# Two-layer decoder trunk on one Trainium2 core: the least used expert comes last, its 64 high and 64 low token parts in one stationary block

## What is computed

```python
def moe_swiglu(h, w_router, w_gate, w_up, w_down):
    logits = (x @ w_router).astype(jnp.float32)
    top_logit, top_idx = lax.top_k(logits, TOP_K)          # TOP_K = 2 of N_EXPERTS = 8
    gates = jax.nn.softmax(top_logit, axis=-1)
    ...
    return swiglu(xb, w_gate[e], w_up[e], w_down[e])       # (silu(h @ w_gate) * (h @ w_up)) @ w_down
```

## Time and profile before

| | |
|---|---|
| median of 3 runs | 1447.54 us (1447.46 to 1451.54) |
| profiled execution | 1448.84 us, of which the span of instructions 1447.0 us |
| PE busy | 1417.0 us, 98% of the span |
| DVE, ACT, POOL busy | 1116.4 us (77%), 944.6 us (65%), 52.8 us (4%) |
| 336 expert slots: DVE subtract, ACT copy | 2286 ns and 1915 ns each |
| DMA in the expert stage | 346 to 398 GB/s by slices of 36 us |
| indirect stores of token rows, issue to landing | 10.4 us |

### The profile page before, as it was taken

How to read it: one execution, slowest core, us unless ns; L and a number is a source line. 1 busy time by engine, 2 the same in 40 slices (tenths; PEclk the granted TensorE clock), 3 DMA queues, 4 the chain that set the end, 5 groups by cost and what they waited for, 6 DMA issues and landing times.

```text
span 1447.0 us, 19532 instructions
## 1 busy us (share of the span) xinstructions
PE 1417.0 (98%) x7348; PEld 1201.7 (83%) x7348; DVE 1116.4 (77%) x865; ACT 944.6 (65%) x866; POOL 52.8 (4%) x78
## 2 busy tenths in 40 slices
PE   8999999999998999999999999999999999999997
PEld 8887999998887888888888888888888888888886
DVE  5565544546775888798888889879888888987987
ACT  5654544335664867787677777767768768677774
POOL 1000100000000500000000000000000000000002
PEclk9999999999999899999999999999999999999999
DMA  9743665555531699999999999999999999999993
GB/s 283 265 146 116 252 228 187 193 191 177 185 117 59 213 397 395 397 393 395 393 354 395 396 346 394 398 349 392 396 391 347 395 393 346 393 398 352 396 396 136
DMA packets 205253, 446.72 MB, mean 309 GB/s; under 512 B 8448, under 2 KB 42400, under 8 KB 205200
## 3 DMA queue, kind: packets, MB, share of 16 engines
q1 hardware_dynamic: 200144, 428.34, 80.5%
q0 software_dynamic: 5056, 17.66, 3.5%
HBM read 432.86 MB, written 13.11 MB: 308 GB/s over the span
## 4 chain that ended last, share of the span: by engine, by line
PE 90%; DVE 3%; ACT 3%; DMA 2%; issue 1%; SPq 1%; DVEq 0%; ACTq 0%
PE ps L1686 28%; PE ps L1688 28%; PE ps L1687 28%; PE ps L2300 2%; DMA raw<-in_w_exp_down_dram 1%; DMA raw<-in_w_mem_kv_dram 1%; ACT w_hi L593 1%; ACT e_whi L977 1%; DVE w_lo L1058 1%; PE ps L2243 0%; PE ps L1835 0%; PE ps L2294 0%; ACT sc L637 0%; DVE small L1105 0%; PE ps L1712 0%
## 5 line engine op out<-in xcount | busy, mean ns | idle before, releaser
L1567 DVE TENSOR_TENSOR e_wlo<-raw,e_whi 128x2048 fp32r<-128x2048 f32 x336 | 752.6, 2286 | 103.0 <-ACT e_whi L977 102.9
L977 ACT ACTIVATE e_whi<-raw 128x2048 fp32r<-128x2048 f32 x336 | 622.9, 1915 | 53.2 <-PE ps L1688 26.2
L1686 PE MATMUL ps<-e_whi,act_hi 128*128 128x512 f32 x1344 | 529.4, 394 | 0.7 <-DVE act_lo L1580 0.7
L1688 PE MATMUL ps<-e_wlo,act_hi 128*128 128x512 f32 x1344 | 523.9, 390 | 0.0
L1687 PE MATMUL ps<-e_whi,act_lo 128*128 128x512 f32 x1344 | 523.2, 389 | 0.0
L1688 PEld LDWEIGHTS ps<-e_wlo,act_hi 128*128 128x128 f32 x1344 | 252.3, 188 | 53.3
L1686 PEld LDWEIGHTS ps<-e_whi,act_hi 128*128 128x128 f32 x1344 | 252.4, 188 | 52.0 <-DVE e_wlo L1567 1.4
L1687 PEld LDWEIGHTS ps<-e_whi,act_lo 128*128 128x128 f32 x1344 | 252.6, 188 | 50.6
L1058 DVE TENSOR_TENSOR w_lo<-raw,w_hi 128x2048 fp32r<-128x2048 f32 (+3 forms) x69 | 148.7, 2167 | 118.8 <-ACT w_hi L593 118.5
L593 ACT ACTIVATE w_hi<-raw 128x2048 fp32r<-128x2048 f32 (+3 forms) x69 | 124.3, 1816 | 47.2 <-PE ps L1688 43.5
L982 ACT ACTIVATE act_hi<-ps 128x512 fp32r<-128x512 f32 x56 | 33.5, 598 | 155.2 <-PE ps L2300 155.2
(11 more groups left out here) (270 smaller groups left out, 966.1 us busy)
## 6 DMA issues: line engine op xcount, KB each, us to landing
raw<-in_w_exp_gate_dram SPq DMA_DIRECT2D x112, 1024.0 KB, 9.3
raw<-in_w_exp_up_dram SPq DMA_DIRECT2D x112, 1024.0 KB, 9.5
raw<-in_w_exp_down_dram SPq DMA_DIRECT2D x112, 1024.0 KB, 10.1
raw<-in_w_dense_gate_dram SPq DMA_DIRECT2D x11, 1024.0 KB, 5.3
raw<-in_w_dense_up_dram SPq DMA_DIRECT2D x11, 1024.0 KB, 5.6
raw<-in_w_dense_down_dram SPq DMA_DIRECT2D x11, 1024.0 KB, 6.7
raw<-in_w_out_dram SPq DMA_DIRECT2D x8, 1024.0 KB, 5.0
raw<-in_w_in_a_dram SPq DMA_DIRECT2D x7, 1024.0 KB, 11.9
```

Of the source, the lines that this page charges most:

```text
L977: nc.scalar.activation(e_whi[:, (s - NPRE) % E_SPLIT, :], raw[:, s % RAW, :], ACT.Copy)\
L1567: nc.vector.tensor_tensor(e_wlo[:, r, :], raw[:, s % RAW, :], e_whi[:, r, :].bitcast(F32), ALU.subtract).then_inc(lo_ready, 1)
L1686: nc.tensor.matmul(dst, l_hi, r_hi, start=start, stop=False)
L1688: return nc.tensor.matmul(dst, l_hi, r_lo, start=False, stop=stop)
```

## The change

- After the counts are known, DVE sorts the experts: expert 0 stays first, the others follow by falling count (`order_of`, `place`). SP reads the number of the next expert from SBUF before it issues that expert's loads; POOL's row numbers use `place`, so they wait for `routed` in place of `ranked`. If the last expert has over 64 tokens, its ranks from 64 on are moved past 128, so that the second sweep runs.
- The last expert (`light`) has its at most 64 tokens' high parts in stationary columns 0 to 63 and their low parts in columns 64 to 127 (`pack`). Each product is then two matmuls of 512 columns, times the high and the low weights. Rows 0 to 63 and 64 to 127 of the result are its two halves, to be summed.
- For the hidden block the sum is made in the turning: ACT copies the gate product and DVE the up product to SBUF, and PE multiplies both with `fold` (two 64-wide identities, one on the other), 8 matmuls of 64 columns (`light_turn`). ACT takes the silu of the turned gate, DVE multiplies by the turned up part, ACT writes the high part, DVE the low part beside it. For the output the sum is made in the scatter, whose one-hot columns stand twice.

The diff, cut to its core:

```diff
         h_hi, h_lo = ([buf[:, 4 * i:4 * i + 4, P:S] for i in range(2)] for buf in (act_hi, act_lo))
+        e_u, s_T, h_T = (H[:, 1, a:b] for a, b in ((0, 512), (512, 768), (768, 1024)))
+        scratch = sb("scratch", [P, NE * NE])
 
...
+                if sweep == 0:
+                    loads(0, 0)
+                    sp.wait_ge(routed, 1)
+                    with sp.Fori(1, NE) as e:
+                        loads(e, sp.value_load(order_of[0:1, bass.ds(e, 1)], min_val=0, max_val=NE - 1))
+                else:
+                    with sp.Fori(0, NE) as e:
...
-            iota8 = cst[:, C_IOTA:C_IOTA + NE].rearrange("p (o e) -> p o e", o=1).to_broadcast([P, TT, NE])
+            pool.wait_ge(routed, 1)
+            place_of = place.rearrange("p (o e) -> p o e", o=1).to_broadcast([P, TT, NE])
             nc.gpsimd.tensor_scalar(row1, route_rank[:, :, :], P - 0.5, 1.0e6, ALU.is_gt, ALU.mult)
-            link(nc.gpsimd.tensor_scalar(row_of, iota8, float(P), None, ALU.mult))
+            link(nc.gpsimd.tensor_scalar(row_of, place_of, float(P), None, ALU.mult))
...
+                def light_silu(e, j):
+                    act.wait_ge(e_tr, e * STEPS + j + 1)
+                    nc.scalar.activation(s_T, ps[:, 4, 0:256], ACT.Silu)\
+                      .then_inc(l_silu, 1)
+
+                def light_high(e, j):
+                    act.wait_ge(l_prod, j + 1)
+                    nc.scalar.activation(h_hi[j % 2][:, :, 0:LIGHT], h_T.rearrange("p (m n) -> p m n", m=4), ACT.Copy)\
+                      .then_inc(e_hi, 1)
...
                         else:
                             split_slots(e, gate_end(j) + 2, 2)
-                            hidden(e, j - 1)
+                            (light_silu if light else hidden)(e, j - 1)
                         if j == 2 and (sweep or last):
                             act.wait_ge(oh_turned, e + 2 if sweep else 1)
                             nc.scalar.activation(ohT[:, :], ps[:, 7, 0:256], ACT.Copy).then_inc(ohT_ready, 1)
                         act.wait_ge(slot_used, e * PER_EXPERT + base + gate_end(j))
-                        nc.scalar.activation(e_h[:, :], ps[:, j % 2, :], ACT.Silu).then_inc(e_silu, 1)
+                        nc.scalar.activation(e_h[:, :], ps[:, j % 2, :], ACT.Copy if light else ACT.Silu).then_inc(e_silu, 1)
+                        if light and j > 0:
+                            light_high(e, j - 1)
 
...
                 nc.vector.reciprocal(rt[:, 4:6], rt[:, 4:6]).then_inc(gate_inverse, 1)
                 dve.wait_ge(totals, 1)
-                link(nc.vector.tensor_reduce(rt[:, 24:25], ps[:, 4, 0:NE], AX.X, ALU.max))
+                count, key, sorted8, past = ps[:, 4, 0:NE], rt[:, 8:16], rt[:, 16:24], rt[:, 32:40]
+                above = scratch[:, :].rearrange("p (e f) -> p e f", e=NE)
+                late = scratch[:, 0:TT * NE].rearrange("p (t e) -> p t e", t=TT)
+                link(nc.vector.scalar_tensor_tensor(out=key, in0=count, scalar=float(NE), in1=cst[:, C_IOTA:C_IOTA + NE],
+                                                    op0=ALU.mult, op1=ALU.add))
+                link(nc.vector.tensor_scalar(key[:, 0:1], key[:, 0:1], 1.0e6, None, ALU.add))
+                link(nc.vector.max(sorted8, key))
+                link(nc.vector.max_index(order_of, sorted8, key))
+                link(nc.vector.tensor_tensor(above, key.rearrange("p (o e) -> p o e", o=1).to_broadcast([P, NE, NE]),
+                                             key.rearrange("p (e o) -> p e o", o=1).to_broadcast([P, NE, NE]), ALU.is_gt))
+                link(nc.vector.tensor_reduce(place, above, AX.X, ALU.add))
+                link(nc.vector.tensor_scalar(is_light, place, NE - 1.5, None, ALU.is_gt))
+                link(nc.vector.tensor_scalar(late, route_rank[:, :, :], LIGHT - 0.5, float(P - LIGHT), ALU.is_gt, ALU.mult))
+                link(nc.vector.tensor_tensor(late, late, light_column(), ALU.mult))
+                link(nc.vector.tensor_tensor(route_rank[:, :, :], route_rank[:, :, :], late, ALU.add))
+                link(nc.vector.tensor_scalar(past, count, LIGHT + 0.5, float(P - LIGHT), ALU.is_gt, ALU.mult))
+                link(nc.vector.tensor_tensor(past, past, is_light, ALU.mult))
+                link(nc.vector.tensor_tensor(past, past, count, ALU.add))
+                link(nc.vector.tensor_reduce(rt[:, 24:25], past, AX.X, ALU.max))
                 nc.vector.tensor_copy(flag[0:1, 0:1], rt[0:1, 24:25]).then_inc(routed, 1)
+
+            def light_column():
+
+                return is_light.rearrange("p (o e) -> p o e", o=1).to_broadcast([P, TT, NE])
+
+            def of_light(dst, table):
+
+                picked = scratch[:, 0:TT * NE].rearrange("p (t e) -> p t e", t=TT)
+                link(nc.vector.tensor_tensor(picked, table, light_column(), ALU.mult))
+                return nc.vector.tensor_reduce(dst, picked, AX.X, ALU.add)
 
...
+                def light_product(j):
+                    dve.wait_ge(l_silu, j + 1)
+                    nc.vector.tensor_tensor(h_T, s_T, ps[:, 4, 256:512], ALU.mult)\
+                      .then_inc(l_prod, 1)
+
+                def light_low(e, j):
+                    dve.wait_ge(e_hi, e * STEPS + j + 1)
+                    nc.vector.tensor_tensor(h_hi[j % 2][:, :, LIGHT:P], h_T.rearrange("p (m n) -> p m n", m=4),
+                                            h_hi[j % 2][:, :, 0:LIGHT].bitcast(F32), ALU.subtract).then_inc(e_lo, 1)
+
+                def pack(half):
+
+                    dve.wait_ge(xg_l, 2 * (NE - 1) + half + 1)
+                    ks = slice(4 * half, 4 * half + 4)
+                    nc.vector.tensor_copy(xg_hi[:, ks, LIGHT:P], xg_lo[:, ks, 0:LIGHT].bitcast(F32)).then_inc(xg_packed, 1)
...
+                        if j == 0 and light:
+                            of_light(cur_rank, route_rank[:, :, :]).then_inc(cur_done, 1)
                             dve.wait_ge(cur_done, 1)
-                            one_hot(0)
+                            twice = cst[:, C_IOTA:C_IOTA + LIGHT].rearrange("p (o n) -> p o n", o=1).to_broadcast([P, 2, LIGHT])
+                            for t in range(TT):
+                                nc.vector.tensor_scalar(oh[:, t, :].rearrange("p (c n) -> p c n", c=2), twice,
+                                                        cur_rank[:, t:t + 1], None, ALU.is_equal).then_inc(oh_ready, 1)
...
+                        if j > 0 and light:
+                            split_slots(e, gate_end(j) + 2, 2)
+                            light_product(j - 1)
+                            split_slots(e, gate_end(j + 1) - 2, 1)
+                            light_low(e, j - 1)
+                            split_slots(e, gate_end(j + 1) - 1, 1)
+                        elif j == 1:
...
                         dve.wait_ge(slot_used, e * PER_EXPERT + base + gate_end(j) + 2)
-                        nc.vector.tensor_tensor(e_h[:, :], e_h[:, :], ps[:, 2 + j % 2, :], ALU.mult).then_inc(e_hr, 1)
+                        if light:
+                            nc.vector.tensor_copy(e_u, ps[:, 2 + j % 2, :]).then_inc(e_hr, 1)
+                        else:
+                            dve.wait_ge(e_silu, (e + done) * STEPS + j + 1)
+                            nc.vector.tensor_tensor(e_h[:, :], e_h[:, :], ps[:, 2 + j % 2, :], ALU.mult).then_inc(e_hr, 1)
                         if j == STEPS - 1 and sweep == 0 and last:
                             add_rows(0, 0)
...
             over = dve.value_load(flag[0:1, 0:1], min_val=0, max_val=S)
-            last_gates = cur_gate.rearrange("p (t o) -> p t o", o=1)
+            end_gates = rt[:, 26:28]
+            link(of_light(end_gates, route_gate[:, :, 1:NE + 1]))
             with dve.If(over > P):
                 remainder_y(NE)
...
+                def light_product(e, u0, bank, first=False):
+
+                    for half in range(2):
+                        hi, lo = slot(e, u0 + half, 4, 512)
+                        if first:
+                            pe.wait_ge(xg_packed, half + 1)
+                        for kk in range(4):
+                            k = 4 * half + kk
+                            nc.tensor.matmul(bank, xg_hi[:, k, :], hi[:, kk, :], start=k == 0, stop=False)
+                            ins = nc.tensor.matmul(bank, xg_hi[:, k, :], lo[:, kk, :], start=False, stop=k == KT - 1)
+                        ins.then_inc(slot_used, 1)
+
+                def light_turn(e, j):
+
+                    pe.wait_ge(e_silu, e * STEPS + j + 1)
+                    pe.wait_ge(e_hr, e * STEPS + j + 1)
+                    for i, src in enumerate((e_h, e_u)):
+                        for m in range(4):
+                            to = 256 * i + LIGHT * m
+                            ins = nc.tensor.matmul(ps[:, 4, to:to + LIGHT], src[:, P * m:P * m + P], fold, start=True, stop=True)
+                    ins.then_inc(e_tr, 1)
+
...
+                def light_expert(e):
+
```

(63 more changed lines are left out.)

42 lines of the change are left out of this document (25 added, 17 removed).

## The result

The changed kernel takes **1460.61 us** (median of 4 runs, 1459.01 to 1462.24) where the kernel before, on the same chip, takes 1447.7 us (median of 4). The ratio is 1.0086, 95% interval 1.0073 to 1.0098: 12.9 us slower. The forecast was 1455.5 us, range 1449.5 to 1463.5.

A forecast was written before the change was run, and what follows sets the result against it. PE was taken as the bound, with DVE tied to ACT setting the last expert's pace afterwards. 2.9 + 2.9 + 0.6 + 0.5 - 0.4 + 1.5 = +8.0 us on the median 1447.54 gave 1455.5 us, range 1449.5 to 1463.5.

The forecast's parts named there:

- likeliest case: Whole kernel: the forecast itself, 1455.5 us, by its bounds 1452 to 1459 us; chance 0.59.
- PE freed, DVE next: Last expert: PE, the bound, loses 168 matmuls, 38 us; DVE with ACT then sets the pace.
- Part 1, routing, +2.9: First expert's slot 2: 15 short DVE instructions replace two, delaying PE, which never makes it good; +2.9 us.
- The covers: Routing: POOL's rows land by 543 us, before SP asks at 553.15; SP's seven expert-number readings cost 0.
- Part 2, entry, 1.8 us earlier: Last expert's start: first gate product has 16 matmuls, not 24, so ACT and DVE start 1.8 us earlier.
- Part 3, the loop: Last expert's six steps: DVE tied to ACT, 16.8 us each, 100.8 in all; closing of step 6 +2.9 us.
- Part 4, the tail, +0.6: Last closing instruction to end of last low part: 3.3 us with a 1.0 us fold, against 2.7; +0.6 us.
- Part 4, gates and branch, +0.5: Kernel's end: the last expert's gate becomes a masked sum of two linked instructions ahead of the branch; +0.5 us.
- Part 4, the second half, -0.4: Output's low part: DVE no longer waits 0.40 us for its second half; -0.4 us.
- Part 5, the clock, +1.5: PE at half clock after stands, at slot 2 and the last scatter: +1.5 us, bounds 0 and 3.5.
- The clock rival: Last expert: half clock through most of PE's work, steps about 1 us longer, 1459 to 1464 us; chance 0.10.
- The faster rival: Last expert: ACT and DVE not tied, a step 14.6 us, kernel 1441.3 us; chance 0.10.

The follow-up runs named there:

- The order alone: Changed kernel with the last expert back at three matmuls a group, sort and new expert order kept: 1452.01 us, against 1448.17 for the kernel before.
- the early sort: Changed kernel with DVE's sort instructions moved ahead into its waits around slot 1 of the first gathering: 1455.69 us, ratio 1.0053 to the kernel before.
- the kernel with 18 constant matmuls: Changed kernel plus constant PE matmuls: 30 in step 1, 18 in steps 2 to 6, 16 ahead of the scatter: 1457.44 us.
- the last version: Changed kernel with ACT exchange, early sort, earlier gate sum, earlier cuts of slots 4 and 5, plus 18, 9 and 6 constant matmuls: 1445.81 us.
- the last two versions: Changed kernel with ACT exchange, early sort, earlier gate sum and earlier cuts of slots 4 and 5: without constant matmuls 1447.05 us, with them 1445.81 us.

## Why the prediction was right

Its sign, its likeliest case and its mechanism held, and 1460.61 us lies in the range, but the point was 5.1 us low. Some 2.6 us of that are terms of the sum (8.0 against 10.6 between the spans). The other 2.5 are how far the profiled executions stood from the medians, and belong to no step of the prediction. By its own parts:

- **PE freed, DVE next: right.** The 38 us taken from PE turned mainly into 19.7 us of standing at the down product, 4.0 at the scatter, the fold matmuls (1.9 us in each of seven turnings, in place of 0.44) and matmuls at half clock. The foretold stand of 4.9 us a step was not seen: the stands are 7.1, 2.1, 2.2, 2.2, 2.2 and 3.8 us. The fold is 0.9 us longer than priced, and half clock takes some 1.5 us more of the same gap (7 or 8 matmuls at 0.43 us, not 0.23).
- **Part 1, routing, +2.9: 1.8 us.** The chain of short instructions was sized rightly (2.8 us at the cut of slot 2, 2.6 us of standing by PE). What failed is "since it waits for nobody later, it never makes it good". PE had waited 0.7 us for a low part before, inside the first expert, where loads still set the pace; in the kernel after that wait is gone, and with it about 1 us of the delay. The order alone showed 1.8 us both at the first and at the last closing. The covers held: POOL was done at 523.84, 9 us ahead of the 532.5 worked out, SP read at 553.63, 0.5 us later than before, and its seven readings of an expert's number cost nothing to be seen.
- **Part 2, entry, 1.8 us earlier: right.** The delay of 1.8 and this gain cancel: the closing of step 0 starts at 1330.51 against 1330.57.
- **Part 3, the loop: right.** Foretold 16.8 us a step with a stand of 2.2 behind each product; measured 16.85 with 2.29 in five steps of six. The one of 17.56 us is half clock: its product waited 0.45 us for ACT's late silu, and with full clock that step took 16.85 us too. In the sum the six steps were +4.8 us and measured +5.8. The exchange of two instructions in ACT's queue gave steps of 14.5 and 14.7 us, which proves the tie and gives its price, 8.9 us over six steps.
- **Part 4, the tail, +0.6: +3.2.** This is the step that was mis-sized most. It has two parts. The fold was taken as 1.0 us by eight matmuls of 64 columns, but those rows are eight records, and a float32 matmul here leaves two. The rows of the kernel after, at full clock, in its first turning:

```profile
1332.60 1.00 PE L2420 MATMUL ps<-w_r,e_h 128*128 128x64 f32 x8
1333.44 1.06 PE L2420 MATMUL ps<-w_r,H 128*128 128x64 f32 x8
```

  Eight matmuls are 16 records and 1.9 us (1332.60 to 1334.50); at half clock, in the last turning, they took 2.7 us. At full clock, with constant matmuls ahead of it, the stretch took 4.6 us, so 1.3 us of the excess are the fold and the handovers, and 1.4 us the clock. Inside the steps the same term did no harm, since PE stood there anyway.
- **Part 4, gates and branch, +0.5: +0.8**; the gap before the copy grew from 2.52 us to 3.07 us, and was 2.50 us once the masked sum no longer stood ahead of the branch. It was 2.87 us in three of the kernels above with the sum still there, so part of the growth is not steady.
- **Part 4, the second half, -0.4: nothing gained.** DVE's two halves of the low part are one row of two, with no wait between, as written. But DVE's next instruction then waits for PE's scatter, 0.79 us here and 0.3 us in the two kernels whose scatter followed a stand of only 1.6 us, at full clock (the exchange and the early sort). In those two the stretch to the end is 11.3 us, as before the change. The 0.8 us more of the kernel after are thus half clock in the scatter. In the kernel with 18 constant matmuls, also at full clock, it is 11.5 us.
- **Part 5, the clock, +1.5: some 3 us.** The total lies inside the bounds of 0 to 3.5, but its places were others. Slot 2, priced at 1.5 us, cost nothing; its window shows the clock still whole:

```profile
493.00:494.00 1.00, 0.00 (x0) 1.00 0.03 8
```

  Instead the last turning and fold cost 1.4 us, the steps 0.7, and the scatter 0.6 to 0.8 (priced at up to 1.8). By the rule of the Trainium skill (TensorE: Matmul & The Clock Gate, "HAM oscillation — how this bites in real kernels") every burst after a stand starts cold, that is at half clock. The trace agrees only in part: of the six down products two start at half clock, three fall to it 1.1 to 1.4 us after their start, and one stays at 1.00. It also shows that half clock in a burst costs what the next engine notices of it, here 0.7 us in six steps.

Corrected by these sizes the sum is 1.8 - 1.8 + 5.8 + 3.2 + 0.8 + 0.8 = +10.6 us, the clock being contained in its stretches. The wrongs of the routing (too much) and of the tail (too little) partly cancelled. The clock rival named 1459 to 1464 us, where the time in fact lies, but not by its mechanism: it wanted steps 1 us longer each, and one step was 0.7 longer. The faster rival failed by the very order that was named against it. When that order was removed it met two limits that it had not priced in full: the late turning at half clock, and DMA.

## What to carry to other kernels

When work is taken from the bounding engine, write out the next engine's step as a loop with its waits for the others: two engines that each have idle time in a step (DVE worked 14.6 of 16.85 us here) can be tied to the full step by one instruction that stands ahead of a cut in a queue. Exchanging the two gave back 8.9 us in the six steps here and 9.8 us in all. A gain in one stage can't exceed the room to the next limit; here DMA's 15.8 us a step against PE's 16.8 left about 6 us for six steps besides what the raw ring holds, so 38 us of matmuls were never to be had. Count the short chain at the end of a kernel by records of the very operation, at the clock it will have there, since nothing covers it.

## What the runs showed of the hardware

- A float32 matmul of 128 by 128 on 128 columns leaves two records and takes 0.23 us (34 in 7.76 us); one on 64 columns takes 0.24 us (8 in 1.9 us). Rows of such matmuls must be halved before they are used as a price.
- PE's granted clock fell to 0.50 during stands of 3.8, 4.0 and 7.1 us. Behind stands of 2.1 to 2.2 us it fell in three of four cases, 1.1 to 1.4 us after PE had begun again, and behind one of 2.6 us it did not. It was back 4 to 5 us after PE had begun again. With 30 and 18 constant matmuls put into the stands it was 1.00 through the last expert; with 18 and 9 in the last version it was 0.56 to 0.59 from 1400 to 1404 us and 0.53 to 0.62 from 1424 to 1428.
- Reading the flag and branching took DVE 2.50 to 2.52 us where other work stood ahead of it (the kernel before and the last two versions). With the two linked instructions right ahead it took 2.87 us in three kernels and 3.03 to 3.07 us in three others. Why was not tried.
